# Expert activations in a mixture-of-experts kernel: transposed by VectorE in 32 x 32 blocks instead of by TensorE

## The chip, the cores and the metric

One core of one Trainium2 chip runs the whole kernel. The metric is the device time of one execution in microseconds (us). It was run three times before the change; the median counts.

## What is computed

The reference is a two-layer decoder trunk on 256 tokens of width 1024, all in float32. The change touches only the last part of the second layer, an expert SwiGLU in which every token goes to 2 of 8 experts:

```
logits = h @ w_router;  top_v, top_i = top_k(logits, 2);  gate = softmax(top_v)
for e in range(8):
    out += comb[:, e] * ((silu(h @ wg[e]) * (h @ wu[e])) @ wd[e])     # wg, wu: 1024 x 3584, wd: 3584 x 1024
```

All eight experts' weights, 8 x 3 x 14.7 MB, are read from memory once.

## The kernel before

The work of the expert part is cut into items: one item is one expert with up to 96 token slots (`CAP`), three pieces of 32 (`PIECE`). This input has 8 items. An item has 7 steps (`MOE_STEPS`) of 512 hidden columns, so there are 56 steps. A step `n` is, in the order in which TensorE (PE) issues it (`item` in the PE block):

1. `up_e` for the gate columns (`kind` 0), then for the up columns (`kind` 1). For each of 8 blocks `k` of 128 input channels, the 32 slots of one piece are the stationary operand and the weights, 128 x 512, are the moving operand. TensorE's array is used in four column groups of 32: the output's partitions choose the group. Groups 0 to 2 take one piece each with the first 384 weight columns (L1420). Group 3 takes the last 128 weight columns for all three pieces, one matmul each (L1423).
2. `down_e` of the step before (`n - 1`): four blocks `c` of hidden channels, two halves of the output, with the same split into groups (L1390 and L1394). It reads `a_T`, the activations with hidden channels on partitions.
3. `turn(n)`: three PE transposes of `hid_tok[:, 1]`, 128 x 128 each, into PSUM bank 4 (L1382), which use the whole array. ScalarE (ACT) copies the bank into `a_T` in `turned` (L801).

At step 3 of an item and at step 1 of the first, small matmuls (`info`, L1368) follow on the whole array. At step 6 of an item the next item's rows are transposed between the ups and the down (`turn_rows`, L1374).

ScalarE computes `silu` of bank 0 into `hid_tok[:, 0]` (L828), and VectorE (DVE) multiplies it with bank 1 into `hid_tok[:, 1]` (`multiply`, L2061). Semaphores `f_silu` and `f_mul` count these, `w_used[0]`, `w_used[1]` and `w_used[2]` count finished gate, up and down blocks on PE, `mt_done` the PE transposes and `ma_done` the filled `a_T`. Besides `multiply`, DVE makes the next item's one-hot rows at step 2 and at step 4 the row numbers `take_next` (L2085), with which GpSimd (POOL) gathers the next item's rows from memory.

Weights come by DMAs of 2 MB that SyncE (SP) issues in order (L339 for gate and up into a ring of 7 buffers, L334 for down into 3 buffers), each as soon as `w_used` says that its buffer is free. Three of them serve one step.

In the trace a float32 matmul stands as two MATMUL and two LDWEIGHTS records. One `k` or one `c` of one output half is therefore two rounds of three matmuls on group 3 and one each on groups 0 to 2: 32 rounds in the two ups of a step, 16 in its down.

Of the kernel before, what the change touches and what calls it, by code (L numbers as in the profile page):

```python
# [84 lines left out]
def build(nc, x_d, mem_d, wl_d, wf_d, wm_d, small_d, const_d, router_d, gfin_d, out_d):  # L85
    ctx = ExitStack()
    with ctx:
# [5 lines left out]
        def sem(name):  # L93
            return ctx.enter_context(nc.semaphore(name))
# [90 lines left out]
        def bank(i):  # L185
            return PS[:, i, :]
# [57 lines left out]
        down_landed = [w_in_ring[2], sem("down_landed1"), sem("down_landed2")]  # L244
        ring_in = [w_in_ring[0]] + [sem(f"ring_in{i}") for i in range(1, RING)]
        oh_ready, gath_done, e_ready = sem("oh_ready"), sem("gath_done"), sem("e_ready")
        mt_done, ma_done = sem("mt_done"), sem("ma_done")
        md_moved = sem("md_moved")
        md_hi, md_lo, ohT_done, ohT_ready, sc_done = sem("md_hi"), sem("md_lo"), sem("ohT_done"), sem("ohT_ready"), sem("sc_done")
        exp_table, s_half, nm_half, exps_half = sem("exp_table"), sem("s_half"), sem("nm_half"), sem("exps_half")  # L250
# [228 lines left out]
        def _(act):  # L479
# [316 lines left out]
                nc.scalar.activation(junk[:, t, half], x[:, t, half], ACT.Square,  # L796
                                     accum_out=stat[:, 64 + 2 * hf + t:65 + 2 * hf + t]).then_inc(f_ssq, 1)

            def turned(n):
                act.wait_ge(mt_done, n)  # L800
                nc.scalar.activation(a_T[:], bank(4)[:, 0:3 * P], ACT.Copy).then_inc(ma_done, 1)  # L801

            def item(it, first=False):
                for s in range(MOE_STEPS):
                    n = it * MOE_STEPS + s
                    begin = first and s == 0
                    if s == 0:
                        for b in range(2):
                            act.wait_ge(gath_done, it * 2 + (b + 1))
                            for k in range(4 * b, 4 * b + 4):  # L810
                                ins = nc.scalar.activation(e_in[:, k, :], bank(6 + b)[:, (k % 4) * P:(k % 4) * P + P], ACT.Copy,
                                                           scale=sml("g_ffn", k, k + 1))
                            ins.then_inc(e_ready, 1)
                    if begin:
                        act.wait_ge(pos_done, 2)
                        for t in range(NT):
                            normed(t)
                        act.wait_ge(rv, RV_DIF)
                        nc.scalar.activation(rt[:, 260:262], rt[:, 258:260], ACT.Exp).then_inc(r_exp, 1)
                    else:  # L820
                        turned(n)
                        if s == 1 and not first:
                            act.wait_ge(w_used[2], it * MOE_STEPS + MOE_USED[2])
                            rows_of(it)
                    act.wait_ge(w_used[0], n + (MOE_USED[0] + 1))
                    if not begin:
                        act.wait_ge(f_mul, n + FF_STEPS)
                    nc.scalar.activation(hid_tok[:, 0, :], bank(0)[:, 0:3 * P], ACT.Silu).then_inc(f_silu, 1)  # L828
                    if s == 1 and not first:
                        rest_of(it)  # L830
# [4 lines left out]
            with act.Fori(1, n_items) as it:  # L835
                item(it)
            steps = n_items * MOE_STEPS
            turned(steps)
            act.wait_ge(ohT_done, 1)
            nc.scalar.activation(onehot_T[:], bank(5)[:, 0:SEQ], ACT.Copy).then_inc(ohT_ready, 1)  # L840
            act.wait_ge(ohT_done, 2)
# [17 lines left out]
        def _(pe):  # L859
# [515 lines left out]
                    if k % 4 == 3:  # L1375
                        ins.then_inc(gath_done, 1)

            def turn(n):

                pe.wait_ge(f_mul, n + (FF_STEPS + 1))  # L1380
                for c in range(3):
                    ins = nc.tensor.transpose(bank(4)[:, c * P:(c + 1) * P], hid_tok[:, 1, c * P:(c + 1) * P], ident)  # L1382
                ins.then_inc(mt_done, 1)

            def down_half(s, hf, start, stop):
                w, cols = down_ring[DOWN_SLOT[s]], hf * 512
                for c in range(4):
                    for t in range(3):
                        a = a_T[:, c * P + t * PIECE:c * P + (t + 1) * PIECE] if c < 3 else a_T[:, t * P + CAP:(t + 1) * P]
                        mm(bank(2 + hf)[t * PIECE:(t + 1) * PIECE, 0:HALF], a, w[:, c, cols:cols + HALF],  # L1390
                           start=(start and c == 0), stop=(stop and c == 3), skip_group_check=True)
                    for t in range(3):
                        a = a_T[:, c * P + t * PIECE:c * P + (t + 1) * PIECE] if c < 3 else a_T[:, t * P + CAP:(t + 1) * P]
                        ins = mm(bank(2 + hf)[CAP:P, t * P:(t + 1) * P], a, w[:, c, cols + HALF:cols + 512],  # L1394
                                 start=(start and c == 0 and t == 0), stop=(stop and c == 3), skip_group_check=True)
                return ins
# [8 lines left out]
            def up_e(it, s, kind, first):  # L1405
                p, n = 2 * s + kind, it * MOE_STEPS + s
                r, turn_ = p % RING, p // RING
                if r == 0:
                    pe.wait_ge(ring_in[0], it * 32 + (MOE_FILLS[0] + turn_ + 1) * 16)
                else:  # L1410
                    pe.wait_ge(ring_in[r], it * 32 + (turn_ + 1) * 16)
                if not (first and s == 0):
                    pe.wait_ge(f_mul if kind else f_silu, n + FF_STEPS)
                w = ring[r]
                for k in range(KD):
                    if kind == 0 and s == 0 and k % 4 == 0:
                        pe.wait_ge(e_ready, it * 2 + (k // 4 + 1))
                    for t in range(3):
                        rows = slice(t * PIECE, (t + 1) * PIECE)
                        mm(bank(kind)[rows, 0:3 * P], e_in[:, k, rows], w[:, k, 0:3 * P], start=(k == 0), stop=(k == KD - 1),  # L1420
                           skip_group_check=True)
                    for t in range(3):
                        ins = mm(bank(kind)[CAP:P, t * P:(t + 1) * P], e_in[:, k, t * PIECE:(t + 1) * PIECE], w[:, k, 3 * P:4 * P],  # L1423
                                 start=(k == 0 and t == 0), stop=(k == KD - 1), skip_group_check=True)
                ins.then_inc(w_used[kind], 1)

            def item(it, first=False):
                for s in range(MOE_STEPS):
                    n = it * MOE_STEPS + s
                    begin = first and s == 0  # L1430
                    if begin:
                        pe.wait_ge(gt_ready, 1)
                        info(slice(0, 3))
                        keep_busy(3, 12)
                    for kind in range(2):
                        up_e(it, s, kind, first)
                    if s == MOE_STEPS - 1:
                        turn_rows(it + 1)
                    if not begin:
                        if s == 1 and not first:  # L1440
                            pe.wait_ge(md_hi, it * 2 - 1)
                        down_e(it if s else it - 1, (s - 1) % MOE_STEPS, n - 1)
                    turn(n)
                    if first and s == 1:
                        pe.wait_ge(gt_ready, 2)
                        info(slice(3, 4))
                    if s == 3:
                        pe.wait_ge(oh_ready, it + 2)
                        info(slice(0, 4))
# [47 lines left out]
        def _(dve):  # L1497
# [559 lines left out]
            def multiply(n):  # L2057
# [2 lines left out]
                dve.wait_ge(w_used[1], n + (MOE_USED[1] + 1))  # L2060
                V.tensor_tensor(hid_tok[:, 1, :], bank(1)[:, 0:3 * P], hid_tok[:, 0, :], ALU.mult).then_inc(f_mul, 1)  # L2061

            def item(it, first=False):
                for s in range(MOE_STEPS):
                    n = it * MOE_STEPS + s
                    multiply(n)
                    if first and s == 2:
                        dve.wait_ge(info_done, 2)
                        V.tensor_copy(gate_slot, bank(5)[:, 3:4]).then_inc(put_ready, 1)
                    if s == 2:  # L2070
                        if not first:
                            dve.wait_ge(put_done, it * 16 + 32)
                            V.tensor_copy(put_now[:], put_next[:])
                            V.tensor_copy(gate_slot, info_next[:, 3:4]).then_inc(put_ready, 1)
                        dve.wait_ge(info_done, it + 2)
                        onehots(it + 1)
                        gate_of(it + 1, oh_ready)
                    if s == 4:
                        dve.wait_ge(info_done, it + 3)
                        V.tensor_copy(info_next[:], bank(5)[:, 0:4]).then_inc(row_done, 1)  # L2080
                        dve.wait_ge(row_done, it * 2 + 3)
                        slots_of()
                        dve.wait_ge(row_done, it * 2 + 4)
                        V.tensor_scalar(put_next[:], row_f[:], spare, None, ALU.add)
                        V.tensor_copy(take_next[:], info_next[:, 0:1]).then_inc(take_ready, 1)  # L2085
# [154 lines left out]
```

## Time and profile before

| | us |
|---|---|
| three runs, median (lowest to highest) | 1599.73 (1598.84 to 1601.5) |
| the profiled execution, own time | 1602.24 |
| its span, first to last instruction | 1600.4 |
| mean granted clock of TensorE, share of full | 0.994 |
| PE busy in the span | 1573.4 (98%) |
| DVE busy, ACT busy | 463.5 (29%), 396.7 (25%) |
| expert part, from about 650 us to the end | some 950 |

PE is busy nearly all the time. A busy PE is not PE at its peak, since its matmuls overlap; how many instructions fit into a stretch says more than the busy share. An engine's idle time is named with what ended it.

### The profile page before, as it was taken

Reading aid. Unit: us, or ns where it says so; the run is one execution under the profiler, and the core shown is the slowest. Engines: PE = TensorE matmul, PEld = TensorE weight load, DVE = VectorE, ACT = ScalarE, POOL = GpSimd, SP = SyncE. Lnnn points to the kernel's source line nnn. Section 1 sums busy time; section 2 is a strip of 40 time slices with the busy share of each in tenths; the row PEclk is TensorE's granted clock in tenths of the full one; section 3 lists DMA queues with packets and bytes.
Section 4 is the critical chain, followed back from the end, with each engine's and each line's share of the span. In section 5 each row is a group of like instructions: output and inputs, shape, how many; then the busy total and the mean of one; then the engine's idle time right before and its main releaser. Section 6 shows DMA issues by size and latency. Waiting matters only on the chain.

```text
span 1600.4 us, 43531 instructions
## 1 busy us (share of the span) xinstructions
PE 1573.4 (98%) x20165; PEld 1451.4 (91%) x20165; DVE 463.5 (29%) x688; ACT 396.7 (25%) x669; POOL 41.2 (3%) x63
## 2 busy tenths in 40 slices
PE   9999999999999999899999999999999999999997
PEld 8778888888887888899999999999999999999996
DVE  5857556666666764200000000000000000000002
ACT  6644444434565443100101101101001101101001
POOL 1000000000000000000000000000000000000000
PEclk9999999999999999999999999999999999999998
DMA  8524335555443446999999999999999999999941
GB/s 334 211 100 164 132 116 210 183 192 195 173 185 124 165 158 277 377 426 418 380 417 382 378 418 383 365 425 358 394 415 362 402 396 377 401 396 377 410 155 76
DMA packets 41192, 472.44 MB, mean 295 GB/s; under 512 B 4816, under 2 KB 6432, under 8 KB 11456
## 3 DMA queue, kind: packets, MB, share of 16 engines
q1 hardware_dynamic: 35280, 454.33, 70.6%
q0 software_dynamic: 3632, 13.58, 2.7%
q8 instruction: 155, 2.54, 0.6%
q10 hardware_dynamic: 2112, 1.88, 0.4%
q14 instruction: 13, 0.11, 0.0%
HBM read 463.18 MB, written 5.90 MB: 293 GB/s over the span
## 4 chain that ended last, share of the span: by engine, by line
PE 94%; DMA 3%; DVE 1%; issue 1%; ACT 1%; POOL 0%; POOLq 0%; DVEq 0%; SPq 0%
PE PS L1423 22%; PE PS L1420 14%; PE PS L1394 12%; PE PS L1153 9%; PE PS L1390 7%; PE PS L864 6%; PE PS L866 5%; PE PS L865 5%; PE PS L1154 5%; PE PS L1382 2%; DMA w1v<-wl_dram 1%; PE PS L1215 1%; PE PS L1195 1%; PE PS L936 1%; DMA x_rows<-x_normed 1%
## 5 line engine op out<-in xcount | busy, mean ns | idle before, releaser
L1423 PE MATMUL PS<-ring,e_in 128*32 128x128 f32 x5376 | 599.2, 273 | 0.0
L1420 PE MATMUL PS<-ring,e_in 128*32 128x384 f32 x5376 | 591.1, 488 | 4.7 <-DMA ring<-wm_dram 4.7
L1423 PEld LDWEIGHTS PS<-ring,e_in 128*32 128x32 f32 x5376 | 583.4, 110 | 0.4
L1394 PE MATMUL PS<-down,a_T 128*32 128x128 f32 x2688 | 304.0, 273 | 0.0
L1390 PE MATMUL PS<-down,a_T 128*32 128x384 f32 x2688 | 300.7, 488 | 0.0
L1394 PEld LDWEIGHTS PS<-down,a_T 128*32 128x32 f32 x2688 | 293.7, 110 | 0.4
L2061 DVE TENSOR_TENSOR hid_tok<-PS,hid_tok 128x384 f32<-128x384 f32 x56 | 31.2, 557 | 851.8 <-PE PS L1423 851.8
L1420 PEld LDWEIGHTS PS<-ring,e_in 128*32 128x32 f32 x5376 | 214.8, 109 | 13.1 <-issue 7.9
L1502 DVE TENSOR_TENSOR wlo<-stage,whi 128x2048 fp32r<-128x2048 f32 (+2 forms) x55 | 171.9, 3127 | 94.1 <-ACT whi L483 94.1
L483 ACT ACTIVATE whi<-stage 128x2048 fp32r<-128x2048 f32 (+2 forms) x57 | 148.4, 2608 | 94.6 <-PE PS L866 52.2
L1153 PE MATMUL PS<-pairB,whi 128*128 128x512 f32 x480 | 168.9, 396 | 0.5 <-DVE pairB L1836 0.5
L801 ACT ACTIVATE a_T<-PS 128x384 f32<-128x384 f32 x56 | 27.3, 488 | 471.7 <-PE PS L1382 471.7
L1154 PE MATMUL PS<-pairB,wlo 128*128 128x256 f32 x480 | 134.6, 280 | 0.0
L1153 PEld LDWEIGHTS PS<-pairB,whi 128*128 128x128 f32 x480 | 90.0, 188 | 22.1 <-issue 0.8
L1390 PEld LDWEIGHTS PS<-down,a_T 128*32 128x32 f32 x2688 | 107.7, 109 | 1.3 <-issue 1.3
L1154 PEld LDWEIGHTS PS<-pairB,wlo 128*128 128x128 f32 x480 | 90.7, 189 | 0.4
L828 ACT ACTIVATE hid_tok<-PS 128x384 f32<-128x384 f32 x56 | 27.5, 491 | 255.7 <-PE PS L1423 255.7
L864 PE MATMUL PS<-whi,pairB 128*128 128x454 f32 (+1 forms) x192 | 73.3, 382 | 0.3 <-DVE pairB L1597 0.3
L866 PE MATMUL PS<-whi,pairB 128*128 128x454 f32 (+1 forms) x192 | 72.0, 375 | 0.0
L865 PE MATMUL PS<-wlo,pairB 128*128 128x454 f32 (+1 forms) x192 | 72.0, 375 | 0.0
L864 PE MATMUL PS<-whi,pairA 128*128 128x512 f32 x128 | 51.2, 400 | 0.6 <-DVE wlo L1502 0.6
L866 PE MATMUL PS<-whi,pairA 128*128 128x512 f32 x128 | 49.9, 390 | 0.0
(354 smaller groups left out, 1448.9 us busy)
## 6 DMA issues: line engine op xcount, KB each, us to landing
ring<-wm_dram SPq DMA_DIRECT2D x112, 2048.0 KB, 13.5
down<-wm_dram SPq DMA_DIRECT2D x56, 2048.0 KB, 14.2
stage<-wl_dram SPq DMA_DIRECT2D x20, 2048.0 KB, 7.5
stage<-wf_dram SPq DMA_DIRECT2D x33, 1024.0 KB, 4.8
stage<-wl_dram SPq DMA_DIRECT2D x4, 1816.0 KB, 8.0
w1k<-wl_dram SPq DMA_DIRECT2D x2, 2048.0 KB, 8.0
w1v<-wl_dram SPq DMA_DIRECT2D x2, 2048.0 KB, 7.9
third<-wl_dram SPq DMA_DIRECT2D x2, 1816.0 KB, 8.9
```

The costliest lines, as they stand in the source:

```text
L483: nc.scalar.activation(whi[slot][:, 0:n], (raw or stage[slot])[:, 0:n], ACT.Copy).then_inc(w_hi[slot], 1)
L864: mm(out, ah, bh, start=start, stop=False)
L865: mm(out, ah, bl, start=False, stop=False)
L866: return mm(out, al, bh, start=False, stop=stop)
L1153: mm(out, wh, pair[:, :, k, :], start=(k == 0), stop=False, skip_group_check=True)
L1154: return mm(out[:, 0, :], wl, pair[:, 0, k, :], start=False, stop=(k == KD - 1), skip_group_check=True)
L1382: ins = nc.tensor.transpose(bank(4)[:, c * P:(c + 1) * P], hid_tok[:, 1, c * P:(c + 1) * P], ident)
L1390: mm(bank(2 + hf)[t * PIECE:(t + 1) * PIECE, 0:HALF], a, w[:, c, cols:cols + HALF], start=(start and c == 0), stop=(stop and c == 3), skip ...
L1394: ins = mm(bank(2 + hf)[CAP:P, t * P:(t + 1) * P], a, w[:, c, cols + HALF:cols + 512], start=(start and c == 0 and t == 0), stop=(stop and ...
L1420: mm(bank(kind)[rows, 0:3 * P], e_in[:, k, rows], w[:, k, 0:3 * P], start=(k == 0), stop=(k == KD - 1), skip_group_check=True)
L1423: ins = mm(bank(kind)[CAP:P, t * P:(t + 1) * P], e_in[:, k, t * PIECE:(t + 1) * PIECE], w[:, k, 3 * P:4 * P], start=(k == 0 and t == 0), s ...
L1502: V.tensor_tensor(wlo[slot][:, 0:n], (raw or stage[slot])[:, 0:n], f32(whi[slot][:, 0:n]), ALU.subtract).then_inc(w_lo[slot], 1)
```

## The change

PE no longer transposes the activations. VectorE does it, with one instruction of 128 x 384 that transposes each block of 32 x 32 in its place. For this the up stage writes its output in another layout: each column group `g` takes a quarter of the weight columns (those with `g * 32` to `g * 32 + 31` in each block of 128) for all three pieces of slots. The three PE transposes, the ScalarE copy and the semaphore `mt_done` are gone. `down_half` reads `a_T` at other offsets and is otherwise the same.

```diff
@@ semaphores
-        mt_done, ma_done = sem("mt_done"), sem("ma_done")
+        ma_done = sem("ma_done")
@@ ScalarE
-            def turned(n):
-                act.wait_ge(mt_done, n)
-                nc.scalar.activation(a_T[:], bank(4)[:, 0:3 * P], ACT.Copy).then_inc(ma_done, 1)
...
-                        turned(n)
...
-            turned(steps)
@@ PE, down_half (both places)
-                        a = a_T[:, c * P + t * PIECE:c * P + (t + 1) * PIECE] if c < 3 else a_T[:, t * P + CAP:(t + 1) * P]
+                        a = a_T[:, t * P + c * PIECE:t * P + (c + 1) * PIECE]
@@ PE, turn
-            def turn(n):
-
-                pe.wait_ge(f_mul, n + (FF_STEPS + 1))
-                for c in range(3):
-                    ins = nc.tensor.transpose(bank(4)[:, c * P:(c + 1) * P], hid_tok[:, 1, c * P:(c + 1) * P], ident)
-                ins.then_inc(mt_done, 1)
...
-                    turn(n)
@@ PE, up_e
                     for t in range(3):
-                        rows = slice(t * PIECE, (t + 1) * PIECE)
-                        mm(bank(kind)[rows, 0:3 * P], e_in[:, k, rows], w[:, k, 0:3 * P], start=(k == 0), stop=(k == KD - 1),
-                           skip_group_check=True)
-                    for t in range(3):
-                        ins = mm(bank(kind)[CAP:P, t * P:(t + 1) * P], e_in[:, k, t * PIECE:(t + 1) * PIECE], w[:, k, 3 * P:4 * P],
-                                 start=(k == 0 and t == 0), stop=(k == KD - 1), skip_group_check=True)
+                        for g in range(4):
+                            ins = mm(bank(kind)[g * PIECE:(g + 1) * PIECE, t * P:(t + 1) * P], e_in[:, k, t * PIECE:(t + 1) * PIECE],
+                                     w[:, k, :].rearrange("p (c g j) -> p g c j", c=4, g=4)[:, g], start=(k == 0 and t == 0), stop=(k == KD - 1),
+                                     skip_group_check=True)
@@ DVE
+            def turn(n):
+                dve.wait_ge(f_mul, n + (FF_STEPS + 1))
+                dve.wait_ge(w_used[2], n + MOE_USED[2])
+                V.transpose(a_T[:], hid_tok[:, 1, :]).then_inc(ma_done, 1)
+
             def item(it, first=False):
                 for s in range(MOE_STEPS):
                     n = it * MOE_STEPS + s
+                    if not (first and s == 0):
+                        dve.wait_ge(ma_done, n)
                     multiply(n)
+                    turn(n)
```

## Rows read from the trace of the kernel before

**Rows 1.** The page, busy us of each engine, share of the span, instructions

```profile
PE 1573.4 (98%) x20165; PEld 1451.4 (91%) x20165; DVE 463.5 (29%) x688; ACT 396.7 (25%) x669; POOL 41.2 (3%) x63
```

**Rows 2.** Windows: stretch, busy PE, PEld, DVE, ACT, POOL (count), clock, DMA share, GB/s

```profile
669.00:672.50 3.50, 3.50 (x36) 3.12 (x40) 0.00 (x0) 0.00 (x0) 0.00 (x0) 0.52 1.02 435
800.00:1500.00 700.00, 700.00 (x12392) 683.33 (x12385) 31.23 (x96) 67.03 (x152) 18.87 (x26) 1.00 0.97 392
673.00:722.00 49.00, 49.00 (x877) 48.20 (x873) 2.17 (x7) 2.95 (x6) 0.00 (x0) 1.00 1.01 426
```

**Rows 3.** Groups by line, 700 to 1590 us: busy us, mean ns, idle before

```profile
L1423 PE MATMUL PS<-ring,e_in 128*32 128x128 f32 x5076 | 564.0, 273 | 0.0
...
L1394 PE MATMUL PS<-down,a_T 128*32 128x128 f32 x2592 | 293.2, 273 | 0.0
...
L1382 PE MATMUL PS<-const,hid_tok 128*128 128x128 f32 x159 | 29.0, 291 | 0.0
```

**Rows 4.** Timeline of DVE, 1007 to 1090 us: start, us, instruction, idle before

```profile
1007.73 0.56 DVE L2061 TENSOR_TENSOR hid_tok<-PS,hid_tok 128x384 f32<-128x384 f32 x1 [16.94 <-PE PS L1423]
1024.06 0.56 DVE L2061 TENSOR_TENSOR hid_tok<-PS,hid_tok 128x384 f32<-128x384 f32 x1 [15.78 <-PE PS L1423]
...
1056.73 0.56 DVE L2061 TENSOR_TENSOR hid_tok<-PS,hid_tok 128x384 f32<-128x384 f32 x1 [12.95 <-PE PS L1423]
1073.41 0.56 DVE L2061 TENSOR_TENSOR hid_tok<-PS,hid_tok 128x384 f32<-128x384 f32 x1 [16.12 <-PE PS L1423]
...
1074.46 0.14 DVE L2085 CAST take_next<-info_next 128x1 int32<-128x1 f32 x1
```

**Rows 5.** Timeline of PE and its weight loads, one step from 1013 us

```profile
1013.29 0.52 PE L1423 MATMUL PS<-ring,e_in 128*32 128x128 f32 x3
...
1028.48 0.71 PE L1394 MATMUL PS<-down,a_T 128*32 128x128 f32 x5
1029.12 0.55 PE L1382 MATMUL PS<-const,hid_tok 128*128 128x128 f32 x3
1029.60 0.52 PE L1420 MATMUL PS<-ring,e_in 128*32 128x384 f32 x3
...
1029.12 0.31 PEld L1382 LDWEIGHTS PS<-const,hid_tok 128*128 128x128 f32 x3 [0.20 <-issue]
```

**Rows 6.** Timeline of PE at an item's step 3

```profile
945.94 0.55 PE L1382 MATMUL PS<-const,hid_tok 128*128 128x128 f32 x3
946.33 0.51 PE L1368 MATMUL PS<-info_tok,onehot 128*128 128x4 f32 x4
```

**Rows 7.** Two lines' weight loads: ns min/median/max, first and last start us

```profile
L1041 PEld LDWEIGHTS PS<-const,z x32: 133/136/138, 54.9 to 55.8; 128*64 128x64 f32 x32
...
L1308 PEld LDWEIGHTS PS<-router_g,xT x16: 190/192/192, 633.1 to 634.7; 128*128 128x128 f32 x16
```

**Rows 8.** Timeline, small or grouped matmuls in other stages

```profile
54.89 1.03 PEld L1041 LDWEIGHTS PS<-const,z 128*64 128x64 f32 x32 [0.31 <-issue]
...
64.64 0.41 PE L1075 MATMUL PS<-w1k,blk_T 128*32 128x256 f32 x2
...
66.15 0.41 PE L1075 MATMUL PS<-w1k,blk_T 128*32 128x256 f32 x2
...
55.99 1.04 PE L903 MATMUL PS<-causal_bf,ident_bf 128*128 128x512 bf16 x4
```

**Rows 9.** Timeline of PE, second step of the first item

```profile
668.94 0.69 PE L1420 MATMUL PS<-ring,e_in 128*32 128x384 f32 x3 [4.72 <-DMA ring<-wm_dram]
```

**Rows 10.** The page: a DMA queue; issue groups with KB each, us to landing

```profile
q8 instruction: 155, 2.54, 0.6%
...
ring<-wm_dram SPq DMA_DIRECT2D x112, 2048.0 KB, 13.5
...
xg<-x_rows,take_next POOLq DMA_INDIRECT x8, 10.7
```

**Rows 11.** The chain that ended last, near its end

```profile
1576.27 3.08 issue
```

More of the change, by code:

```diff
@@ L1392, in down_half @@
                     for t in range(3):
-                        a = a_T[:, c * P + t * PIECE:c * P + (t + 1) * PIECE] if c < 3 else a_T[:, t * P + CAP:(t + 1) * P]
+                        a = a_T[:, t * P + c * PIECE:t * P + (c + 1) * PIECE]
                         ins = mm(bank(2 + hf)[CAP:P, t * P:(t + 1) * P], a, w[:, c, cols + HALF:cols + 512],
```

## The prediction

> **What bounds the kernel now.** I read the page first. PE is busy for 1573 of 1600 us and no other engine for a third of the span [rows 1]. The windows then show what a change to the expert part can touch: over 700 us of it PE has not one idle microsecond at a granted clock of 1.00, while the DMA engines are 97% busy [rows 2]. So a step costs what PE's instructions take, and DMA has to be watched as the next bound. The groups by line show which instructions these are: ups, downs and three transposes a step (L1382) [rows 3]. The timeline of DVE is the step's clock, since the multiply follows each pair of ups: 1007.73 to 1024.06 is 16.33 us, and a step with `info` takes 16.68 (1056.73 to 1073.41) [rows 4].
>
> **What paces the ups and downs.** In an ordinary step group 3's first matmul starts at 1013.29. Of the down's last five, which end at 1029.19 (28.48 + 0.71), the last starts one mean duration of 273 ns earlier, at 1028.92 [rows 3, 5]. Between the two lie 143 gaps (48 rounds of 3 matmuls, less one), so 15.63 / 143 = 109.3 ns each: 128 columns at two passes and 2.4 GHz are 106.7, and 2.6 more. Group 3 is thus never without work, and the round is 3 x 109.3 = 328 ns. Groups 0 to 2 stream 384 columns per round, 320 ns and one such surcharge, so group 3 is the slowest of the four.
>
> **Removed: the transposes on PE.** Group 3's first matmul of the next step would start at 1029.62 (two hundredths after L1420's 1029.60). Without the turn it can start one gap after the down's last, at 1029.03. That saves 0.59 us: 0.48 from the turn's start to the next up (1029.12 to 1029.60), and 0.09 to 0.11 because the weight loads stand idle for 0.20 where the array goes from groups to the whole [rows 5]. With `info` at step 3 (and step 1 of the first item) the change of shape stays, and the saving is the turn alone up to L1368's start, 0.39 us [rows 6]. At step 6 the row transposes come before the down, so there the saving is whole.
>
> An item saves 6 x 0.59 + 0.39 = 3.93 us, seven items 27.5. In the first, the first step's saving is lost: PE then waits 4.72 us for a weight buffer [rows 9], and arriving earlier it waits longer. (From 669 us the clock is granted at its lower level, 1.2 GHz, for 3.5 us after that wait [rows 2], which costs 1.7 us; whether a longer wait stretches this I can't read, so 1.7 us either way goes into the range.) Four steps at 0.59 and two at 0.39 remain, 3.1 us. The sum is 30.6 us.
>
> **Changed: the ups' matmuls.** Each of the four groups gets three matmuls of 128 columns a round, just what group 3 has now. The columns are the same 384 per group. If each group keeps group 3's pace of 109.3 ns, the round stays 328 ns and the change costs nothing; the cover is group 3 itself. What is new is the supply: 12 matmuls and 12 weight loads a round where there were 6 and 6, that is 328 / 24 = 13.7 ns an instruction. No row shows a denser sustained supply. The densest is L1041, 32 loads and 32 matmuls on two groups of 64 columns: (1.03 - 0.136) / 31 = 28.8 ns a pair, 14.4 an instruction [rows 7, 8]. But that stretch has a limit of its own. L1308 loads 128 columns every (634.7 - 633.1) / 15 = 0.107 us, 64 columns would take half, 53, and over two groups 27 [rows 7]. L1041 can be paced by its loads, which then run in both groups at once. Loads of 32 columns take about 27 ns by the same proportion and hide behind 109. I therefore take zero; the bounds are zero and L1041's rate read as the supply's: 24 x 14.4 = 346 ns, 18 a round, over 32 x 56 = 1792 rounds 32 us.
>
> Four groups with a weight load before each matmul do run together: L1075's pairs go from 64.64 to 66.15 in seven rounds of 216 ns, for 213 of 256 columns [rows 8]. And the moving operand now comes in four pieces of 32 columns. L903 reads its 512 columns in pieces too, two or four (a broadcast mask): four of them last 1.04 us, of which some 0.17 is the latency of the last (L1423's 273 ns less 107 of streaming [rows 3]), so 218 ns each against 213 and the surcharge [rows 8]: a break costs next to nothing there. With pieces of 32 no row stands; the bounds are zero and 2.6 ns for each of three more breaks, 7.8 a matmul, 23 a round, 42 us. I take zero, by the nearer row.
>
> The Trainium skill weighs against this part: TensorE: Matmul & The Clock Gate, section "Wait — 56ns, not 53.3ns?", says that the sequencer, where it decodes matmuls itself, needs about 62 ns for each. By it a new round would take 12 x 62 = 744 ns and the kernel would lose some 745 us. The trace disagrees for this run: L1041 has a pair every 28.8 ns [rows 7, 8].
>
> **Added on VectorE.** One transpose of 128 x 384 a step; no row shows one. The nearest, the multiply of the same size, takes 0.56 us [rows 4]; bounds are half and four times that, 0.3 to 2.2. It waits for the down of step n-1, which ends some 5.2 us (16 rounds) after the ups; `a_T` is then read only after the next two ups, 32 rounds or 10.5 us later. Nothing of it is on the path, even at 2.2 us. Behind the waiting transpose DVE's own queue stands. The multiply n+1 comes 10 us later, so it isn't reached. The one-hots of step 2 come 5 us later, but PE reads them after the next step's down, 15 us on. `take_next` at step 4 (1074.46 now [rows 4]) comes some 5.5 us later; PE reads the gathered rows at step 6, some 31 us later now, about 25 then, and the gather needs 10.7 to landing [rows 10]. All hidden. If DVE were over 10 us late, ups would not stop but the down would, which would be seen as PE idle before L1390.
>
> **Removed from ScalarE:** a copy of about 0.5 us a step, never in PE's way, since no PE group shows idle time [rows 3]. Nothing is gained. At the end, the last down needs `a_T` right after the down before it; there PE stands 3.08 us in its own branches anyway [rows 11], longer than a transpose. Semaphores that SP waits for come as before, relative to PE.
>
> **DMA.** A step reads 3 x 2.1 MB. At 15.74 us that is 400 GB/s, where 392 flow now [rows 2]. The stretch 673 to 722 us, when the queue was never empty, gives 426, so there is room, 14.8 us a step. Loads land 13.5 us after issue [rows 10], and a ring buffer is refilled seven ups ahead, three and a half steps. Instructions are read by DMA as well: 2.54 MB in 155 reads [rows 10]. An up's instruction rate rises by two, the step's by 5/3; it stays one read of 16 KB in over 4 us.
>
> **Sum.** The profiled execution has a span of 1600.4 us and takes 1602.2; less 30.6 these become 1569.8 and 1571.6. The median of the runs is 2.5 us below that execution, so the time is 1599.7 - 30.6 = 1569.1 us.
>
> **Rivals.**
>
> *The supply of instructions paces the ups (slower).* Place: PE's sequencer, in the 32 up rounds of each step. L1041's 14.4 ns, or 16 if its whole 1.03 us is divided by 64, is then the sequencer's and not the loads'. Price: at 15, 24 x 15 = 360 ns, 32 more a round, 57 us, net +27: 1626 us (at 14.4 net +1, at 16 net +70). It decides from 30.6 us / 1792 = 17 ns a round, 345 / 24 = 14.4 ns an instruction. For it: the coincidence of 13.7 needed and 14.4 seen at most. Against it: the same figure follows from L1308's loads. Chance 0.14.
>
> *Breaks in the moving operand, or four groups' loads in each other's way, cost a few ns.* A round of 331 to 343 ns takes 5 to 27 us back: 1575 to 1596. For it: 32-column pieces are shown nowhere. Against: L903 and L1075. Chance 0.12.
>
> *The time goes into waits instead (about the same).* PE's 0.59 us a step becomes a wait for weights or for `a_T`. Price: up to the full 30.6 us, 1600. Against: 426 GB/s and 10 us of cover. Chance 0.03.
>
> *Forecast:* 1565 to 1574 (the saving per step 0.64 at most, if no gap is lost at all in a step; 0.48, the turn alone, at least). Chance 0.71.
>
> **Numbers.** The forecast and the second rival hold 0.83, and end at 1596; I let the range go from 1564 to 1597. A difference under 0.2%, 3.2 us, can't be told from none by a measurement of this kernel. Faster: 0.71 + 0.12 and part of the third, 0.84; same: 0.03; slower: 0.13.
>
> **What would show it.** Right: the multiply's starts lie 15.74 us apart, 16.30 with `info`; L1382 and L801 are gone; ups have 12 matmul records per 328 ns of 273 ns each; a DVE transpose of 0.3 to 2.2 us starts some 5 us after each multiply; PE has no idle time between 670 and 1570 us. Wrong: up rounds longer than 330 ns with starts evenly 14 to 15 ns apart (supply), longer matmul records (breaks), PE idle before L1390 (late `a_T`) or before the ups (DMA). The prediction is wrong at its core if the ups' rounds lengthen by 17 ns.

## The result

The changed kernel takes 1856.19 us (median of 4 runs, 1853.14 to 1860.59) where the kernel before takes 1599.72: the ratio is 1.160 (95% interval 1.158 to 1.163), 256 us slower. The forecast was 1569 us.

The page of the profile after, against [rows 1] and [rows 10]: busy time of each engine, the clock and the DMA share in 40 slices, the instruction queue, and the ring loads.

```profile
PE 1628.1 (88%) x30749; PEld 1475.4 (80%) x30749; DVE 494.1 (27%) x744; ACT 370.5 (20%) x613; POOL 41.2 (2%) x63
...
PEclk9999999999999899999999999999999999999998
DMA  7444255445344798787879788789788877877931
...
q8 instruction: 237, 3.88, 0.8%
...
PE 85%; issue 11%; DVE 1%; DMA 1%; ACT 0%; POOL 0%; POOLq 0%; DVEq 0%; SPq 0%
...
ring<-wm_dram SPq DMA_DIRECT2D x112, 2048.0 KB, 9.0
```

PE is no longer busy all the time, and what it waits for is named "issue": neither data nor another engine. There are 237 instruction reads where there were 155. The weights are not late: a ring load lands 9.0 us after issue instead of 13.5.

The groups by line after, 700 to 1840 us, answer to [rows 3]: where PE sat idle.

```profile
L1407 PE MATMUL PS<-ring,e_in 128*32 128x128 f32 x20470 | 636.3, 281 | 169.1 <-issue 168.4
...
L1377 PE MATMUL PS<-down,a_T 128*32 128x384 f32 x2619 | 317.6, 504 | 14.3 <-issue 14.3
L1381 PE MATMUL PS<-down,a_T 128*32 128x128 f32 x2615 | 310.6, 279 | 9.4 <-issue 9.4
...
L2050 DVE STREAM_TRANSPOSE a_T<-hid_tok 128x384 f32<-128x384 f32 x54 | 31.2, 579 | 308.7 <-PE PS L1381 308.7
```

L1407 is the up matmul of the changed kernel, L1377 and L1381 are the down's. The timeline of PE shows what the waits have in common.

```profile
1032.51 3.70 PE L1407 MATMUL PS<-ring,e_in 128*32 128x128 f32 x128 [0.52 <-issue]
1038.45 3.70 PE L1407 MATMUL PS<-ring,e_in 128*32 128x128 f32 x128 [2.23 <-issue]
1044.39 1.39 PE L1407 MATMUL PS<-ring,e_in 128*32 128x128 f32 x41 [2.25 <-issue]
```

Between two of these stalls lie exactly 128 matmuls, with their 128 weight loads 256 instructions. The instruction queue moved 3.88 MB in 237 reads, 16 KB each; if one read holds these 256 instructions, an instruction is 64 bytes. PE runs them in 3.70 us and stands still until 5.94 us have passed. Within such a run the pace is (3.70 - 0.17) / 256 = 13.8 ns an instruction, just what the ups need: while there are instructions, nothing is slow.

The DMA records of the same trace tie the stalls to the reads. Three short windows each hold one read of the instruction queue, and none lies between them (queue q8: reads, MB, share of 16 engines; windows 1030.15 to 1030.25, 1036.15 to 1036.25 and 1042.1 to 1042.2 us):

```profile
q8 instruction: 1, 0.02, 58.8%
q8 instruction: 1, 0.02, 58.8%
q8 instruction: 1, 0.02, 60.4%
```

The second read starts at 1036.18, takes 0.94 us and lands at 1037.12; PE goes on at 1038.45, 1.33 us later. This holds throughout. All 110 waits of this trace that are longer than 0.4 us end 1.2 to 1.6 us after a read has landed (1.4 in the median), and they lie a multiple of 256 matmuls and weight loads apart, or two to six fewer (PE also has register and semaphore instructions, which I did not count and which may make up the rest). Wherever two of these places follow each other by one such block, exactly one read starts between them. The read itself is short, 0.96 us in the median. It starts late: 3.5 us after the first instruction of the block before has run (median; 5% start within 1.1 us, 95% within 4.2). 3.5 + 1.0 + 1.4 are the 5.9 us.

The windows around a stall of 3.07 us, columns as in [rows 2]:

```profile
953.00:954.70 1.70, 1.70 (x64) 1.44 (x55) 0.00 (x0) 0.00 (x0) 0.00 (x0) 1.00 1.02 434
954.70:957.70 3.00, 0.01 (x1) 0.00 (x0) 0.00 (x0) 0.00 (x0) 0.00 (x0) 1.00 0.73 306
957.70:961.10 3.40, 3.33 (x54) 3.11 (x58) 0.56 (x1) 0.00 (x0) 0.00 (x0) 0.59 0.43 87
961.10:964.50 3.40, 3.40 (x62) 3.30 (x56) 0.00 (x0) 0.00 (x0) 0.00 (x0) 0.90 0.86 357
964.50:968.00 3.50, 3.50 (x115) 3.50 (x111) 0.58 (x1) 1.70 (x2) 0.00 (x0) 1.00 0.82 262
```

After it, PE's clock is granted at its lower level of 1.2 GHz for most of 3.4 us (a mean of 0.59): 54 matmuls. The next window, all down, has 62 at a mean of 0.90, about the down's usual pace (96 in 16 x 328 ns), and the last, ups at full clock, has 115. Between 700 and 1815 us the trace has 24 stretches at the lower level, 43 us of full speed lost; the kernel before has none between 700 and 1580 us. So some of the long stalls are paid twice.

**The sum of the loss.** The profiled execution after has a span of 1855.3 us, against 1569.8 forecast for it: 285 to explain. Idle before PE's matmuls in the expert part is 178.5 + 14.3 + 9.4 by the page (the rows above begin only at 700 us), and 2.2 before the row transposes: 204 us, of which the kernel before has 4.7 as its wait for a weight buffer, so 200. There are 128 such waits (110 before L1407, 10 before L1377, 7 before L1381, 1 before the row transposes), and each starts only after the latency of the last matmul, some 0.17 us (273 ns less 107 of streaming), which counts as busy: 22 us. The mean clock is 0.967 against 0.994: 61 us of full speed lost against 10, so 51 more. Together 273; 12 us I can't assign. Of the lower clock's loss after, 43 us lie between 700 and 1815 us, among the stalls. Another 8.5 lie ahead of the expert part, where the clock was at its lower level from 637.5 to 654.6 us (a mean of 0.53 from 637 to 655, against 1.00 before); no run shows whether the change has a part in these.

### The profile page after: what moved, and what is told of

Its sections match the earlier page's. It is cut to its first block, busy times and chain, and to the rows that moved or that the text cites. A ratio compares the mean times of both kernels' runs of the same rounds, so it can differ in the third digit from the quotient of the medians.

```text
span 1855.3 us, 64754 instructions
## 1 busy us (share of the span) xinstructions
PE 1628.1 (88%) x30749; PEld 1475.4 (80%) x30749; DVE 494.1 (27%) x744; ACT 370.5 (20%) x613; POOL 41.2 (2%) x63
## 3 DMA queue, kind: packets, MB, share of 16 engines
q8 instruction: 237, 3.88, 0.8%
## 4 chain that ended last, share of the span: by engine, by line
PE 85%; issue 11%; DVE 1%; DMA 1%; ACT 0%; POOL 0%; POOLq 0%; DVEq 0%; SPq 0%
PE PS L1407 35%; PE PS L1377 9%; PE PS L1381 8%; PE PS L1147 8%; PE PS L858 5%; PE PS L860 5%; PE PS L859 5%; PE PS L1148 4%; DMA w1v<-wl_dram 1%; PE PS L1209 1%; PE PS L1189 1%; PE PS L930 1%; PE PS L864 1%; PE PS L903 0%; DVE wlo L1486 0%
## 5 line engine op out<-in xcount | busy, mean ns | idle before, releaser
L1407 PE MATMUL PS<-ring,e_in 128*32 128x128 f32 x21504 | 668.6, 281 | 178.5 <-issue 177.8
L1407 PEld LDWEIGHTS PS<-ring,e_in 128*32 128x32 f32 x21504 | 623.7, 113 | 211.7 <-issue 210.0
L1377 PE MATMUL PS<-down,a_T 128*32 128x384 f32 x2688 | 325.3, 504 | 14.3 <-issue 14.3
L1381 PE MATMUL PS<-down,a_T 128*32 128x128 f32 x2688 | 318.7, 279 | 9.4 <-issue 9.4
L1381 PEld LDWEIGHTS PS<-down,a_T 128*32 128x32 f32 x2688 | 299.7, 113 | 17.3 <-issue 14.3
L1377 PEld LDWEIGHTS PS<-down,a_T 128*32 128x32 f32 x2688 | 140.8, 112 | 22.0 <-issue 21.7
L2050 DVE STREAM_TRANSPOSE a_T<-hid_tok 128x384 f32<-128x384 f32 x56 | 32.4, 579 | 313.4 <-PE PS L1381 313.4
L859 PE MATMUL PS<-wlo,pairA 128*128 128x512 f32 x128 | 49.9, 390 | 0.0
L1147 PE MATMUL PS<-pairA,whi 128*128 128x512 f32 x128 | 45.3, 398 | 0.0
```

The lines of the kernel that those rows point to most:

```text
L859: mm(out, ah, bl, start=False, stop=False)
L1147: mm(out, wh, pair[:, :, k, :], start=(k == 0), stop=False, skip_group_check=True)
L1407: ins = mm(bank(kind)[g * PIECE:(g + 1) * PIECE, t * P:(t + 1) * P], e_in[:, k, t * PIECE:(t + 1) * PIECE], w[:, k, :].rearrange("p (c g j ...
L2050: V.transpose(a_T[:], hid_tok[:, 1, :]).then_inc(ma_done, 1)
```

## The experiments

Theory 1 was formed on the trace: PE is starved of instructions. Theory 2 says that the moving operand in pieces of 32 columns, or the new layout, is slow. Theory 3 says that VectorE's transpose or the waits around it are slow. Nine kernels were run: e1 to e9. In the code, `...` marks what is left out. Times are beside runs of the kernel before on the same chip, 1598.9 to 1600.6 us in the median. e2 and e5 were run four times and the others once; the four runs of the changed kernel lie within 7.5 us.

| kernel | PE instructions a step, run / in code | weights | reads, MB | us |
|---|---|---|---|---|
| before | 582 / 582 | all | 155, 2.54 | 1600 |
| changed | 960 / 960 | all | 237, 3.88 | 1856 |
| e1, old layout, 12 matmuls a round, three in a row on a group | 966 / 966 | all | 239, 3.92 | 1955 |
| e6, old layout, 12 matmuls a round, in turn | 966 / 966 | all | 239, 3.92 | 1867 |
| e7, old layout, 9 a round | 774 / 774 | all | 197, 3.23 | 1681 |
| e3, changed, columns in one piece | 960 / 960 | all | 237, 3.88 | 1860 |
| e8, changed, ups from a loop | 960 / 576 | all | 155, 2.54 | 1577 |
| e4, changed, loads cut to an eighth | 960 / 960 | 1/8 from the second expert on | 237, 3.88 | 1611 |
| e9, changed, loads in 4 KB packets | 960 / 960 | all | 237, 3.88 | 1870 |
| e2, before without PE transposes | 576 / 576 | all | 153, 2.51 | 1571 |
| e5, changed, gate and up in one matmul | 576 / 576 | all | 153, 2.51 | 1564 |

**e1_split: as many matmuls in the old layout, first try.**

```diff
-                        mm(bank(kind)[rows, 0:3 * P], e_in[:, k, rows], w[:, k, 0:3 * P], start=(k == 0), stop=(k == KD - 1), ...)
+                        for c in range(3):
+                            mm(bank(kind)[rows, c * P:(c + 1) * P], e_in[:, k, rows], w[:, k, c * P:(c + 1) * P], start=(k == 0 and c == 0), ...)
```

> The kernel before, with each matmul of 384 columns in the ups cut into three of 128 columns on the same column group: as many PE instructions in an up as in the changed kernel, but the old layout, the PE transposes and the ScalarE copy stay and VectorE does nothing new. Theory 1 (PE is starved of instructions: each stall falls on a multiple of 256 instructions, which is one 16 KB read): about as slow as the changed kernel, 1840 to 1900 us, with PE stalls of 1 to 3.5 us named issue and some 235 instruction reads instead of 155. Theory 2 (the pieces of 32 columns in the moving operand or the new layout are slow): 1600 to 1605 us. Theory 3 (the VectorE transpose or its waits): 1600 to 1605 us.

Measured: 1955.1 us, outside all three expectations, and with another cause than theory 1's. PE is busy for 98% of the span, the waits named issue are under 18 us in all, and the multiplies lie 22 to 23 us apart:

```profile
1006.64 0.56 DVE L2062 TENSOR_TENSOR hid_tok<-PS,hid_tok 128x384 f32<-128x384 f32 x1 [23.33 <-PE PS L1424]
1029.96 0.56 DVE L2062 TENSOR_TENSOR hid_tok<-PS,hid_tok 128x384 f32<-128x384 f32 x1 [22.76 <-PE PS L1424]
...
1052.10 0.56 DVE L2062 TENSOR_TENSOR hid_tok<-PS,hid_tok 128x384 f32<-128x384 f32 x1 [21.02 <-PE PS L1424]
```

Here three matmuls in a row go to the same column group, and the groups overlap less. Group 3 (L1424) shows it: its matmuls come 0.11 us apart in runs of six, and then the next one starts only after 0.42 us.

```profile
1000.16 0.27 PE L1424 MATMUL PS<-ring,e_in 128*32 128x128 f32 x1
...
1000.58 0.30 PE L1424 MATMUL PS<-ring,e_in 128*32 128x128 f32 x1
```

The order was changed along with the number, so the run can't decide between the theories. It does show that 239 reads cost next to nothing as such: in a step of 22 to 23 us one is needed every 6 us, and they are nearly always in time.

**e6_rr3: the same number, issued in turn over the groups.**

```diff
...
+                    for c in range(3):
+                        if c < 3:
+                            cols = slice(c * 128, (c + 1) * 128)
+                            for t in range(3):
+                                rows = slice(t * PIECE, (t + 1) * PIECE)
+                                mm(bank(kind)[rows, cols], e_in[:, k, rows], w[:, k, cols], start=(k == 0 and c == 0), ...)
+                        ins = mm(bank(kind)[CAP:P, c * P:(c + 1) * P], e_in[:, k, c * PIECE:(c + 1) * PIECE], w[:, k, 3 * P:4 * P], ...)
```

> The kernel before with the 384 columns of the ups again cut into three matmuls of 128, but issued in turn over the four column groups as in the changed kernel (three in a row on one group was a mistake of the first split). Layout, PE transposes and ScalarE copy as before, 966 PE instructions a step against 960 in the changed kernel and 582 before. Theory 1 (instruction supply): 1830 to 1885 us, with stalls 256 instructions or a multiple apart and some 238 reads. Theories 2 and 3 (column pieces, VectorE): 1600 to 1605 us. If the first split's slowness was the number of matmuls as such: about 1955 us without stalls.

Measured: 1867.4 us, 239 reads. With the old layout, PE's own transposes, no pieces and nothing new on VectorE, the loss is the same. The longest waits, as in the changed kernel:

```profile
PE PS L1423 <- issue: 113.5, 59, 3.6
PE PS L1425 <- issue: 35.5, 20, 3.3
```

Theories 2 and 3 fall here: what the change adds besides the number of instructions is not the cause.

**e7_rr2: in groups 0 to 2, two matmuls of 192 columns instead of three of 128** (against e6; group 3 keeps its three).

```diff
-                        if c < 3:
-                            cols = slice(c * 128, (c + 1) * 128)
+                        if c < 2:
+                            cols = slice(c * 192, (c + 1) * 192)
```

> The same with the 384 columns cut into two matmuls of 192: 774 PE instructions a step, one read of 256 in 4.7 us of the ups instead of 3.5. Theory 1: in the changed kernel a starved read comes every 6.0 us and a step of 3.75 reads took 20.3 us, 5.4 a read; three reads a step are 16.3 us, so it is near the threshold: 1600 to 1680 us, few short stalls. Theories 2 and 3: 1600 to 1603 us.

Measured: 1681.0 us, at the upper end of theory 1's range and just past it. The clock stays at 0.995, and the longest wait in the expert part before its end is 1.8 us. The demand in the ups is then one read in 256 x 18.2 ns = 4.7 us, and this is still too fast.

**e3_contig: the changed kernel with the moving columns in one piece.** The weights' columns are put in the order of the quarters in memory.

```diff
-                                     w[:, k, :].rearrange("p (c g j) -> p g c j", c=4, g=4)[:, g], ...
+                                     w[:, k, g * P:(g + 1) * P], ...
```

> The changed kernel with the gate and up columns ordered by quarters in memory, so that the moving operand is 128 columns in one piece instead of four pieces of 32. Theory 1 (instruction supply): no change, 1850 to 1862 us. Theory 2 (pieces): most of the 256 us come back, below 1620 us.

Measured: 1860.2 us. The pieces cost nothing that this run can show; it is theory 1's expectation, and theory 2's was below 1620.

**e8_loop: as many matmuls, in the same order, from less code.** The products are not the right ones: blocks 1 and 2 stand for 3 to 6 too.

```diff
...
+                block(0)
+                with pe.Fori(0, 3):
+                    block(1)
+                    block(2)
+                block(KD - 1).then_inc(w_used[kind], 1)
```

> The changed kernel, in which the ups run blocks k = 1 and 2 three times from a hardware loop instead of blocks 1 to 6 once. Leaves out the products of blocks 3 to 6 and takes those of 1 and 2 three times. PE executes as many matmuls in the same order, but an up has 192 instructions of code instead of 384. Theory 1: instruction reads fall to about the number before (some 155), stalls nearly vanish, 1570 to 1610 us (what the loop's branches cost is unknown). Against theory 1: unchanged near 1856 us.

Measured: 1577.0 us, 155 reads. PE executes 30749 matmuls, as many as in the changed kernel. The timeline of VectorE, with the multiplies at both ends of an ordinary step:

```profile
1013.31 0.56 DVE L2052 TENSOR_TENSOR hid_tok<-PS,hid_tok 128x384 f32<-128x384 f32 x1 [9.90 <-PE PS L1405]
1018.55 0.58 DVE L2057 STREAM_TRANSPOSE a_T<-hid_tok 128x384 f32<-128x384 f32 x1 [4.68 <-PE PS L1381]
1029.03 0.56 DVE L2052 TENSOR_TENSOR hid_tok<-PS,hid_tok 128x384 f32<-128x384 f32 x1 [9.90 <-PE PS L1405]
```

The step is 15.72 us; the forecast was 15.74. So twelve matmuls a round, pieces of 32 columns and the transpose on VectorE all fit. Only the reading of their code did not. The number of reads fell from 237 to 155, so instructions run again from this loop, 96 of them, were not read again.

**e4_lessdma: weight loads of an eighth.**

```diff
-            def load_up(e, p):
+            def load_up(e, p, w=4096):
...
+                w = 4096 if first else 512
```

> The changed kernel, in which all weight loads from the second expert on bring only the first 512 of 4096 values of each partition (the rest is what the buffer held before), an eighth of the bytes. Leaves out seven eighths of those experts' weights. Theory 1a (an instruction read waits behind the weight reads on its DMA engine): the stalls vanish or shrink to a fraction, 1565 to 1640 us. Theory 1b (an instruction read takes as long without other traffic, about 6 us from request to use): no change, 1840 to 1860 us.

Measured: 1610.7 us. The columns of the waits: engine, line, total us, times, longest. From 820 to 1560 us, with the full-size loads over, there remain:

```profile
PE PS L1408 <- issue: 5.6, 14, 2.5
PE PS L1378 <- issue: 0.6, 1, 0.6
```

and the windows of the same run (columns as in [rows 2]) give the traffic:

```profile
850.00:1550.00 700.00, 693.09 (x20594) 681.46 (x20589) 55.32 (x141) 47.26 (x109) 17.12 (x24) 1.00 0.22 62
```

The changed kernel over a like stretch had 305:

```profile
800.00:1700.00 900.00, 743.82 (x20488) 702.41 (x20481) 54.15 (x138) 47.35 (x109) 17.19 (x24) 0.96 0.81 305
```

At 62 GB/s the same 237 reads arrive nearly in time: what makes a read late is the weight traffic beside it, as theory 1a has it. The DMA records say where the time goes. A read takes 0.98 us here, as long as in the changed kernel (0.96), but it starts 1.1 us (median) after the block before it has begun and not 3.5; the blocks are taken where the changed kernel, whose PE code is the same, stalls. 1.1 + 1.0 + 1.4 are 3.5 us, just what the ups need. So a read waits before it starts, and its transfer is not slower. e4 takes 34 us more than e8. Of these, 18 have come up by the fifth multiply (743.2 us here, 725.3 in e8), during and just after the full-size loads; the other 16 are spread over the rest, of which the waits above show 6.

**e9_desc: weights in packets of 4 KB.** The weights of a load lie in memory as four quarters; 99792 packets on the weight queue instead of 35280.

```diff
+    wm = wm.reshape(E, MOE_STEPS, 3, P, 4, 1024).transpose(0, 1, 2, 4, 3, 5)
...
-                sp.dma_start(ring[p % RING][:].rearrange("p k n -> p (k n)"),
+                sp.dma_start(ring[p % RING][:].rearrange("p (q k) n -> p q (k n)", q=4),
```

> The changed kernel with each 2 MB weight load in 512 pieces of 4 KB instead of 128 of 16 KB (the weights lie in memory as four quarters of 128 partitions). If an instruction read waits behind a number of weight packets already queued on its DMA engine: stalls shrink, 1600 to 1750 us. If it waits for the bytes queued, or its own round trip is what counts: 1840 to 1870 us. DMA itself should stay fast enough, 15 us of it a step.

Measured: 1869.5 us. Smaller packets don't bring the reads in earlier; one starts 3.6 us after the block before it, as in the changed kernel. Behind what a read waits before it starts stays open: this run speaks against a fixed number of packets, and no more.

**e2_noturn: the removal alone.**

```diff
             def turned(n):
-                act.wait_ge(mt_done, n)
-                nc.scalar.activation(a_T[:], bank(4)[:, 0:3 * P], ACT.Copy).then_inc(ma_done, 1)
+                act.wait_ge(f_mul, n + FF_STEPS)
+                act.wait_ge(w_used[2], n - 1 + MOE_USED[2])
+                nc.scalar.activation(a_T[:], hid_tok[:, 1, :], ACT.Copy).then_inc(ma_done, 1)
...
-                    turn(n)
```

> The kernel before without the three PE transposes of a step: ScalarE copies hid_tok[:, 1] into a_T as it stands, at the same place in its order. Leaves out the transposition. This is the removal alone, with the ups as they were. The prediction's term: 30.6 us less, 1569 us (ratio 0.981), a step of 15.74 us and 16.30 with info. If the removed transposes were worth nothing: 1600 us. If PE then waits for a_T or for weights: between the two, with idle time before L1390 or L1420.

Measured: 1570.75 us against 1598.91, ratio 0.982 (0.981 to 0.984), 28.2 us less where the prediction had 30.6. The multiplies, two ordinary steps and then one with `info`:

```profile
1010.87 0.56 DVE L2055 TENSOR_TENSOR hid_tok<-PS,hid_tok 128x384 f32<-128x384 f32 x1 [15.16 <-PE PS L1418]
1026.59 0.56 DVE L2055 TENSOR_TENSOR hid_tok<-PS,hid_tok 128x384 f32<-128x384 f32 x1 [15.16 <-PE PS L1418]
...
1042.31 0.56 DVE L2055 TENSOR_TENSOR hid_tok<-PS,hid_tok 128x384 f32<-128x384 f32 x1 [11.27 <-PE PS L1418]
1058.70 0.56 DVE L2055 TENSOR_TENSOR hid_tok<-PS,hid_tok 128x384 f32<-128x384 f32 x1 [15.84 <-PE PS L1418]
```

**e5_pairs: the change with as few instructions as before.** A load now holds gate and up columns of four blocks `k`, those of a quarter side by side. One matmul of 256 columns gives both, into two banks of PSUM that pieces 0 and 1, and 2, share.

```diff
-                for k in range(KD):
...
+                for k in range(4 * kind, 4 * kind + 4):
...
-                            ins = mm(bank(kind)[g * PIECE:(g + 1) * PIECE, t * P:(t + 1) * P], ...
...
+                            c0 = (k % 4) * 1024 + g * 256
+                            ins = mm(PS[g * PIECE:(g + 1) * PIECE, t // 2, (t % 2) * 256:(t % 2) * 256 + 256], e_in[:, k, t * PIECE:(t + 1) * PIECE],
+                                     w[:, c0:c0 + 256], start=(k == 0 and t != 1), stop=(k == KD - 1), skip_group_check=True)
```

> The changed kernel with gate and up columns of a quarter side by side in memory (a 2 MB load holds four k blocks of both), so that one matmul of 256 columns does what two of 128 did: 192 up matmuls a step instead of 384 in the source, as few PE instructions as before the change, and still no PE transposes. Theory 1 (instruction supply): no stalls; a step of 32 x 3 x 216 ns / 2 for the ups (10.4 us) and 16 x 328 ns for the down (5.25 us), 15.65 us instead of 16.34, so 1560 to 1570 us. Theory 3 (VectorE transpose): stays near 1856 us.

Measured: 1563.98 us against 1600.62, ratio 0.9775 (0.9759 to 0.9791). It beats both kernels, and no wait named issue stands in its expert part but the one at its end. Windows (columns as in [rows 2]) and timeline of VectorE:

```profile
800.00:1500.00 700.00, 700.00 (x12786) 611.05 (x12782) 56.95 (x147) 48.08 (x110) 17.11 (x24) 1.00 1.00 407
```

```profile
1008.96 0.56 DVE L2048 TENSOR_TENSOR hid_tok<-PS,hid_tok 128x384 f32<-128x384 f32 x1 [10.23 <-ACT hid_tok L826]
1013.75 0.58 DVE L2054 STREAM_TRANSPOSE a_T<-hid_tok 128x384 f32<-128x384 f32 x1 [4.23 <-PE PS L1384]
...
1024.56 0.56 DVE L2048 TENSOR_TENSOR hid_tok<-PS,hid_tok 128x384 f32<-128x384 f32 x1 [10.23 <-ACT hid_tok L826]
```

A step is 15.60 us. The 0.12 us under e8's step fit the surcharge of 2.6 ns that half of the up matmuls no longer pay: 16 x 2 x 3 / 2 = 48 fewer per group and step, 0.125 us. Weights now flow at 407 GB/s, and PE is not idle once in these 700 us.

## Why the prediction was wrong

**The removed transposes: right.** The term was 30.6 us and a step of 15.74 us; alone (e2) they gave 28.2 us and a step of 15.72. A step with `info` came down from 16.68 to 16.39 only, not to 16.30, so that saving of 0.39 was sized 0.1 too high. The first step's saving was left out for the weight wait, rightly or not; no run separates it.

**The ups' matmuls: right in what was costed.** Zero for the supply of instructions from PE's sequencer and zero for the pieces: e8 keeps both and has the forecast step. The sequencer hands out an instruction in 13.8 ns or less, so L1041's 14.4 was not its limit; that it was the weight loads' was argued and is not tested. The Trainium skill (TensorE: Matmul & The Clock Gate, "Wait — 56ns, not 53.3ns?") has some 62 ns a matmul where the sequencer decodes matmuls itself. No such pace is seen in this kernel: the timeline after has 128 matmuls in 3.70 us, 28 ns each.

**VectorE: right.** The transpose takes 0.58 us, where the nearest row had 0.56, and starts 4.7 us after the multiply's end in e8. Nobody waits for it.

**The step that failed** is the last sentence of the prediction's part on DMA, "it stays one read of 16 KB in over 4 us". It had the demand on average, and no price for the supply. Two things were missing. The ups ask for a read every 256 x 13.7 = 3.5 us, not every 4.2. And from one block's start to the next one's, with the read between them, PE needs about 6 us under this weight traffic: 5.94 in the rows shown (1032.51, 1038.45, 1044.39), 4.8 to 6.8 over all neighbouring stalls. (Two reads can start closer together: the one at 948.37 comes 3.53 us after the one before it, because the wait before a read's start varies.) Before, the ups ran 256 instructions in 7.0 us, a margin of one microsecond that no wait betrayed. The queue's 0.6% share of DMA time said nothing of it: late reads need no bandwidth. Over a step: 960 instructions are 3.75 reads, at 5.94 us each 22.3 us, near what came (a mean of 21.0 us from the first multiply at 667.5 to the last at 1823.4, against 16.6 before); the 582 before are 2.3 reads, 13.5 us, hidden under 16.3.

**The first rival** had the right place (PE out of instructions in the up rounds), the right sign, and the wrong mechanism and price. It saw a slower even pace, 15 ns an instruction and 1626 us; what came were full pace and stops. It was given 0.14, since all its evidence was on the sequencer's rate and this was indeed no problem. Its own test, starts evenly 14 to 15 ns apart, would have refuted it. A rival on the reads was never written, though their number stood in [rows 10].

**The loss sets in** between 582 and 774 instructions a step: e7, in which only the splitting of the ups is changed, already loses 81 us. The change adds 378.

## What to carry to other kernels

On a fully busy TensorE under heavy weight traffic, count instructions as a resource: 256 of them are one read of 16 KB. Here stretches that used them up in 3.5 and 4.7 us stalled, and one that took 7.0 did not; after some of the long stalls the clock fell too. When a layout needs more and smaller matmuls, look for a neighbour with the same stationary operand to merge them with (e5), or let the code come from a loop (e8), before the transposes saved are booked as a gain. In a profile, the sign is idle time named "issue" at multiples of 128 matmuls with their weight loads, each ending 1.2 to 1.6 us after a read of the instruction queue has landed.

## What the runs showed of the hardware that was not expected

- Instruction reads of 16 KB cost nothing by their share of the DMA time (0.8%), but under 305 GB/s of weight reads each starts 3.5 us (median) after the block before it is entered. With the weights at 62 GB/s it is 1.1, and the same code ran with 6.2 us of waits in 740 us. The transfer takes 1.0 us in both, and PE goes on 1.4 us after it.
- Code run again from a loop of 96 instructions is not read again: 155 reads for 30749 matmuls, against 237 for as many matmuls in straight code.
- The order of the matmuls over the column groups matters. Three matmuls of 128 columns in a row on one group, instead of in turn, made a step of 22 to 23 us (e1); in turn, and with all the stalls, the kernel was still 88 us faster (e6).
- Four column groups keep 109 ns for each matmul of 128 columns with a weight load before each, twelve in 328 ns: e8's step of 15.72 us is 48 such rounds.
